# Seven block products in place of eight for the first sixteen tiles of a feed-forward's down projection

## The chip, the cores and the metric

One core of a Trainium2 chip runs the kernel. The metric is the device time of one execution in microseconds, the median of the runs.

## The reference

One layer of a streaming encoder on x of shape (1, 2048, 1024) in float32: two attention branches, their merge by gates, an output projection, and then the feed-forward that the change is about.

```python
h = _rmsnorm(x, norm1_g[layer])
proj = jnp.einsum('bsd,de->bse', h, w_in[layer])
...
x = x + jnp.einsum('bsd,de->bse', merged, w_out[layer])
h2 = _rmsnorm(x, norm2_g[layer])
ff = jax.nn.silu(jnp.einsum('bsd,df->bsf', h2, w_ffn_gate[layer])) * jnp.einsum('bsd,df->bsf', h2, w_ffn_up[layer])
x = x + jnp.einsum('bsf,fd->bsd', ff, w_ffn_down[layer])
```

D_MODEL is 1024 and D_FF is 2816, which is 22 tiles of 128. Branch B scores all keys for each query, keeps the 256 best and attends to these.

## The kernel before

The sequence is worked in four blocks of 512 rows (NB = 4, ROWS = 512), each four row tiles of 128 (JT = 4). First all four blocks go through `project` (the input projection, in jobs), then each block goes through its attention and its output jobs: branches ("br"), output projection ("wo"), feed-forward.

A **job** is one load of 512 KB of weights and the 24 matmuls that use it. The list JOBS fixes their order for all engines. SyncE loads each job's weights into one of two buffers WRAW. GpSimd splits them into a high and a low half, WHI and WLO (`split`), because every product is computed as three matmuls, high by high, high by low, low by high (the helper `three`). GpSimd may start a job's split when TensorE has finished the job two places before it. Values are split likewise: ScalarE writes the high half, VectorE the low half.

Every engine has its own queue of instructions, written out in the kernel, and takes them in that order: an instruction that waits holds all behind it on its engine.

In the feed-forward, for each tile i TensorE does the gate job "fg" and the up job "fu"; ScalarE applies silu to the first into SL, VectorE multiplies (ff_ready), ScalarE and VectorE split the result into FFhi and FFlo. The 22 tiles are three PARTS of 8, 8 and 6. After the tiles of a part come its down jobs "fd" (`rows`): the values are the stationary operand, and w_down moves in pieces of 512 columns. VectorE adds the sums from PSUM to X1 (`add_row`).

Between these, work for the next block is slipped in: `near` is its near attention, and `search` (VectorE) with `counts` (ScalarE) finds for each row of the next block the threshold of the 256 best scores bit by bit. One **search call** on VectorE takes the counts of the call before, sets the next threshold THR, and counts two of the four row tiles against it; ScalarE counts the other two at the same time. `look` and `next(found)` are such calls, and `search_slots` says how many stand where. A search takes 31 bits, and its calls fall into the output projection and the first two PARTS of the feed-forward of blocks 0, 1 and 2. The last block has no search and no near attention behind it.

In `project`, a scoring unit is two matmuls or four into one of two places of PSUM (LP), a ReLU by ScalarE into RB, and a multiply-add by VectorE. About one unit follows each job of the list SECOND, whose places are called s, from s = 5 on. TensorE must wait for the ReLU of the unit two before.

## Time and profile before

| what | value |
|---|---|
| three runs, us | 3197.46, 3198.58, 3198.94; median 3198.58 |
| span of the profiled execution, from its first to its last instruction | 3196.7 us |
| TensorE busy | 3156.0 us, 99% |
| VectorE, ScalarE, GpSimd busy | 57%, 44%, 64% |
| mean granted TensorE clock | 0.999 |
| matmuls in it | 15678 |

The page gives the span of the profiled execution and no time of its own beside it; the span is 1.9 us under the median of the runs. A busy share is an average over stages: an engine that is busy 57% of the time can still be what another one waits for at one place.

### The profile page before, as it was taken

To read this page: it belongs to the slowest core of one execution; us is meant where nothing else is said; L and a number is where in the kernel's file an instruction comes from. 1 tells how busy PE (TensorE), PEld (TensorE's weight loads), DVE (VectorE), ACT (ScalarE), POOL (GpSimd) and SP (SyncE) were. 2 spreads that over 40 slices of the span, in tenths; PEclk is the share of its full clock that TensorE was granted. 3 is DMA by queue.
4 is the path that set the end of the run, shared out by engine and by line. 5 is a ranking of instruction groups with operands and counts; after the bars stand their busy time and mean duration, and the time that the engine had idled before them with its cause. 6 is when DMAs were issued, how large, how long until landed. Compare 5 with 4: busy or idle time off the path is not lost.

```text
span 3196.7 us, 44024 instructions
## 1 busy us (share of the span) xinstructions
PE 3156.0 (99%) x15678; PEld 2655.0 (83%) x15678; DVE 1814.8 (57%) x3706; ACT 1420.8 (44%) x2589; POOL 2036.0 (64%) x2201
## 2 busy tenths in 40 slices
PE   9999999999999999999999999999999999999998
PEld 7888888878878888888888888988888799888887
DVE  3335546537565545557666666967868689521111
ACT  3324435435473534337354534837655378320001
POOL 5666766665556666764666676366767922666676
PEclk9999999999999999999999999999999999999999
DMA  5765455355615333331533334163333500533332
GB/s 152 198 167 172 119 154 157 103 157 163 209 35 182 102 112 107 108 125 57 201 104 116 103 102 138 28 238 103 98 109 112 171 23 17 180 91 99 95 103 99
DMA packets 464201, 392.59 MB, mean 123 GB/s; under 512 B 29264, under 2 KB 394064, under 8 KB 463344
## 3 DMA queue, kind: packets, MB, share of 16 engines
q1 hardware_dynamic: 442544, 345.56, 36.0%
q10 hardware_dynamic: 21440, 44.22, 3.7%
q8 instruction: 126, 2.06, 0.3%
q14 instruction: 91, 0.75, 0.1%
HBM read 323.76 MB, written 62.81 MB: 121 GB/s over the span
## 4 chain that ended last, share of the span: by engine, by line
PE 92%; POOL 2%; ACT 2%; DVE 2%; issue 1%; DMA 1%; SPq 0%; POOLq 0%; ACTq 0%; DVEq 0%
PE BANK L1049 22%; PE BANK L1051 21%; PE BANK L1050 21%; PE LP L1049 4%; PE LP L1051 4%; PE LP L1050 4%; PE BANK L1330 3%; PE BANK L1355 2%; PE LP L1166 2%; PE LP L1165 2%; PE LP L1310 2%; PE LP L1311 2%; PE BANK L1357 2%; POOL WLO L986 1%; POOL WHI L984 1%
## 5 line engine op out<-in xcount | busy, mean ns | idle before, releaser
L986 POOL TENSOR_TENSOR WLO<-WRAW,WHI 128x512 fp32r<-128x512 f32 x912 | 1213.3, 1330 | 76.0
L984 POOL TENSOR_SCALAR WHI<-WRAW 128x512 fp32r<-128x512 f32 x912 | 639.6, 701 | 776.1 <-PE BANK L1051 622.1
L1049 PE MATMUL BANK<-H2hi,WHI 128*128 128x512 f32 x1376 | 538.7, 392 | 1.1 <-POOL WLO L986 1.1
L1050 PE MATMUL BANK<-H2lo,WHI 128*128 128x512 f32 x1376 | 535.9, 389 | 0.0
L1051 PE MATMUL BANK<-H2hi,WLO 128*128 128x512 f32 x1376 | 535.8, 389 | 0.0
L1049 PE MATMUL BANK<-HThi,WHI 128*128 128x512 f32 (+1 forms) x1024 | 405.1, 396 | 0.8 <-DVE QS L2044 0.5
L1050 PE MATMUL BANK<-HTlo,WHI 128*128 128x512 f32 (+1 forms) x1024 | 399.4, 390 | 0.0
L1051 PE MATMUL BANK<-HThi,WLO 128*128 128x512 f32 (+1 forms) x1024 | 399.3, 390 | 0.0
L1751 ACT ACTIVATE MASK<-SCD,THR 128x896 bf16<-128x896 f32 (+5 forms) x186 | 281.9, 1516 | 191.8 <-DVE THR L2104 164.6
L1051 PEld LDWEIGHTS BANK<-H2hi,WLO 128*128 128x128 f32 x1376 | 258.3, 188 | 54.4
L1049 PEld LDWEIGHTS BANK<-H2hi,WHI 128*128 128x128 f32 x1376 | 258.6, 188 | 53.3 <-issue 1.3
L1050 PEld LDWEIGHTS BANK<-H2lo,WHI 128*128 128x128 f32 x1376 | 258.6, 188 | 51.1
L2071 DVE TENSOR_SCALAR_CACHE_REDUCE MASK<-SCD,THR 128x640 bf16<-128x640 f32 (+2 forms) x192 | 278.1, 1486 | 3.4
L1739 ACT ACTIVATE RB<-LP 128x1024 f32<-128x1024 f32 (+7 forms) x176 | 143.4, 819 | 231.9 <-PE LP L1166 207.9
L2525 DVE TENSOR_TENSOR BANK<-BANK,SL 128x512 f32<-128x512 f32 x88 | 61.2, 696 | 325.7 <-PE BANK L1051 305.9
L2308 DVE SCALAR_TENSOR_TENSOR SCP<-RB,IW,SCP 128x1024 f32<-128x1024 f32 (+7 forms) x140 | 175.2, 1266 | 106.2 <-ACT RB L1739 105.2
L1051 PEld LDWEIGHTS BANK<-HThi,WLO 128*128 128x128 f32 (+1 forms) x1024 | 190.9, 186 | 42.8
L2237 DVE TENSOR_TENSOR PTlo<-BANK,PThi 128x512 fp32r<-128x512 f32 (+1 forms) x296 | 193.2, 659 | 57.5 <-ACT PThi L1680 56.4
L1049 PEld LDWEIGHTS BANK<-HThi,WHI 128*128 128x128 f32 (+1 forms) x1024 | 191.1, 187 | 38.8 <-issue 0.6
L1050 PEld LDWEIGHTS BANK<-HTlo,WHI 128*128 128x128 f32 (+1 forms) x1024 | 191.3, 187 | 36.9
L1633 ACT ACTIVATE LGb<-LGb,NMB 128x1024 f32<-128x1024 f32 (+7 forms) x192 | 174.1, 907 | 57.9 <-POOL NMB L905 54.8
L905 POOL TENSOR_SCALAR NMB<-MXB 128x1 f32<-128x1 f32 x112 | 32.6, 291 | 250.6 <-DVE MXB L2194 247.6
(314 smaller groups left out, 6457.6 us busy)
## 6 DMA issues: line engine op xcount, KB each, us to landing
WRAW<-in_w_in SPq DMA_DIRECT2D x124, 512.0 KB, 4.2
WRAW<-in_w_ffn_gate SPq DMA_DIRECT2D x88, 512.0 KB, 3.8
WRAW<-in_w_ffn_up SPq DMA_DIRECT2D x88, 512.0 KB, 3.8
WRAW<-in_w_ffn_down SPq DMA_DIRECT2D x88, 512.0 KB, 3.5
qsp<-QS SPq DMA_DIRECT2D x32, 512.0 KB, 5.8
WRAW<-in_w_out SPq DMA_DIRECT2D x32, 512.0 KB, 4.6
gates<-GS ACTq DMA_DIRECT2D x62, 256.0 KB, 2.2
GL<-gates ACTq DMA_DIRECT2D x48, 256.0 KB, 4.5
```

Source lines behind the costliest of these rows:

```text
L984: nc.gpsimd.tensor_scalar(hi, raw, 1.0, 1.0, ALU.mult, ALU.mult).then_inc(w_hi, 1)
L986: nc.gpsimd.tensor_tensor(lo, raw, hi.bitcast(f32), ALU.subtract).then_inc(w_split, 1)
L1049: nc.tensor.matmul(dst, whi, mhi, start=first, stop=False)
L1050: nc.tensor.matmul(dst, whi, mlo, start=False, stop=False)
L1051: return nc.tensor.matmul(dst, wlo, mhi, start=False, stop=last)
L1330: last = nc.tensor.transpose(dst[:, 2 * e + h, :], probabilities(b, kind, p, h, t), IDENT[:, :])
L1633: nc.scalar.activation(lg, lg, ACT.Exp, bias=NMB[:, slot, 0:1], accum_out=(ES if s else RS)[:, j, h0:h0 + 1]).then_inc(probs, made(probs, ...
L1739: nc.scalar.activation(RB[:, g % 2, 0:w], logits(("idx",) + key)[:, 0:w], ACT.Relu).then_inc(relu_ready, made(relu_ready, key))
L1751: nc.scalar.activation(mask_of(b)[:, j, 0:w], found_at(b, j)[:, 0:w], ACT.Sign, bias=THR[:, j:j + 1].bitcast(f32), accum_out=CNT[:, j:j + ...
L2071: last = stepped(nc.vector.tensor_scalar(junk[:, j, 0:w], found_at(b, j)[:, 0:w], threshold(j), None, op, ALU.add, accum_out=CNT[:, j:j + 1]))
L2237: nc.vector.tensor_tensor(PTLO[b][r][:, 0:w, :], trans(key)[:, 0:w, :], PTHI[b][r][:, 0:w, :].bitcast(f32), ALU.subtract).then_inc(pt_read ...
L2308: ins = nc.vector.scalar_tensor_tensor(s, r, iw, s, ALU.mult, ALU.add)
```

## The change

It treats the down projection of tiles 0 to 15 as four **quads** of four tiles. In a quad, rows, tiles (even and odd) and columns each fall into two halves, and the 2 x 2 by 2 x 2 block product is formed by seven products in place of eight. Each product is 12 matmuls of the same shape as before. Tiles 16 to 21 keep the old way.

- The products are "11", "t1", "t2", "22", "t3", "21", "t4" in this order. Four of them ("t1" to "t4") use sums of blocks of w_down, which are the same for all four blocks of rows; the other three use w_down itself.
- The sums of weights are formed once, in `project(0)`: for each of eight pairs p of tiles, SyncE loads 1 MB of w_down into DRAW, VectorE forms four sums in DSUM (512 elements per partition each), ScalarE copies their high halves to DHI (2048 elements), VectorE writes the low halves DLO over DSUM, and ScalarE's queue sends both (1 MB each) to DRAM (tsum). The pairs stand at s = 6, 8, ... 20. Pair p + 1 waits for the writes of pair p (dsum_out).
- In the feed-forward the halves of the summed weights are loaded straight into WHI and WLO, 1 MB per product, with no split. A third pair of buffers WHI2, WLO2 is used by the jobs of tiles 0 to 15. Because of the region it lies in, its first split in a block waits for the last "wo" job.
- The sums of the values are formed on GpSimd (`form_sums`): one 256-wide sum for an even tile, three for an odd one. ScalarE and VectorE split these too (`high_parts`, `low_parts`).
- "11", "t2", "t3" and "t4" accumulate on top of one another in LP[0], and "22" on top of "t1" in two banks. VectorE adds each intermediate result to X1 before TensorE may go on with the next one: `down_quad` waits for down_added of "11" before "t2", of "t1" before "22", of "t2" before "t3", of "t3" before "t4".
- The search calls keep their number per part (14), and are placed anew.
- Some semaphores are merged.

```diff
+            def down_quad(b, quad):
...
+                    if x == "t2":
+                        pe.wait_ge(down_added, n(down_added, (b, quad, "11")))
+                        product(x, operand, chain, False)
+                    if x == "22":
+                        pe.wait_ge(down_added, n(down_added, (b, quad, "t1")))
+                        product(x, operand, corner, False)
+                    if x == "t3":
+                        pe.wait_ge(down_added, n(down_added, (b, quad, "t2")))
+                        product(x, operand, chain, False)
...
+                def add_quad(quad, part):
+
+                    add_banks(quad, "t1", (0, 2))
+                    look("fd", part)
+                    add_chain(quad, "t2")
+                    add_banks(quad, "22", (0, 2))
+                    add_chain(quad, "t3")
+                    add_banks(quad, "21", (1, 3))
+                    add_chain(quad, "t4")
...
                         near(b + 1, part_no, at_)
                         next(found, None)
                         near(b + 1, part_no, at_ + 1)
+                        if i // 4 < QUADS and i % 4 == 3:
+                            add_quad(i // 4, part)
```

```diff
+                if key[0] == "wo":
+                    last_out = i
+                third = key[0] == "fs" or key[0] in ("fg", "fu") and key[2] < PARTS[-1][0]
+                w = min((0, 1, 2) if third else (0, 1), key=lambda s: used[s])
+                slot.append(w)
+                before.append(max(used[w], last_out) if w == 2 else used[w])
```

```diff
+            def down_sums(p, step_):
+
+                if step_:
+                    dve.wait_ge(sum_hi, n(sum_hi, ("down", p)))
+                    nc.vector.tensor_tensor(DLO[:, :, :], DSUM[:, :, :], DHI[:, :, :].bitcast(f32), ALU.subtract
+                                            ).then_inc(sum_split, made(sum_split, ("down", p)))
+                    return
+                dve.wait_ge(const_in, n(const_in, ("down", p)))
+                if p:
+                    dve.wait_ge(dsum_out, 32 * p)
...
+                        act.wait_ge(sum_split, n(sum_split, ("down", p)))
+                        c = slice(p % 2 * ROWS, (p % 2 + 1) * ROWS)
+                        for i, half in enumerate((DHI, DLO)):
+                            act.dma_start(io["tsum"][p // 2, :, i, :, c].rearrange("t p c -> p t c"), half[:, :, :].bitcast(f32)
+                                          ).then_inc(dsum_out, 16)
```

The first place is VectorE's queue behind tile 3 of block 0, before the change. L2525 multiplies the up values by the silu, L2528 writes the low half, and the next five rows are a search call.

```order
L2525 TENSOR_TENSOR BANK<-BANK,SL 128x512 [waits silu_ready,bank_full]
L2528 TENSOR_TENSOR FFlo<-BANK,FFhi 128x512 [waits ff_hi]
L2097 TENSOR_SCALAR TAKE<-CNT 128x2 [waits topk_step]
L2101 TENSOR_SCALAR TAKE<-CNT 128x1 [waits tiles_counted]
L2101 TENSOR_SCALAR TAKE<-CNT 128x1
L2104 SCALAR_TENSOR_TENSOR THR<-TAKE,THR 128x4 [waits topk_step]
L2071 TENSOR_SCALAR MASK,CNT<-SCD,THR 128x640 [waits threshold_set]
L2071 TENSOR_SCALAR MASK,CNT<-SCD,THR 128x768
L2525 TENSOR_TENSOR BANK<-BANK,SL 128x512 [waits silu_ready,bank_full]
```

The same place after the change, from the last two 256-wide low halves on; X_237 is X1. L2789 adds LP ("11"), L2800 adds the banks ("t1").

```order
L2763 TENSOR_TENSOR FSlo<-FSUM,FShi 128x256 [waits sum_hi]
L2763 TENSOR_TENSOR FSlo<-FSUM,FShi 128x256
L2789 TENSOR_TENSOR X_237<-LP,X_237 128x2x512 [waits bank_full,rows_added]
L2768 TENSOR_TENSOR FSlo<-SL,FShi 128x512 [waits ff_hi]
L2300 TENSOR_SCALAR TAKE<-CNT 128x2 [waits topk_step]
L2304 TENSOR_SCALAR TAKE<-CNT 128x1 [waits tiles_counted]
L2304 TENSOR_SCALAR TAKE<-CNT 128x1
L2307 SCALAR_TENSOR_TENSOR THR<-TAKE,THR 128x4 [waits topk_step]
L2274 TENSOR_SCALAR MASK,CNT<-SCD,THR 128x640 [waits threshold_set]
L2274 TENSOR_SCALAR MASK,CNT<-SCD,THR 128x768
L2800 TENSOR_TENSOR X_237<-BANK,X_237 128x512 [waits bank_full,rows_added]
L2800 TENSOR_TENSOR X_237<-BANK,X_237 128x512
```

A whole search call now stands between the add of "11" and the add of "t1", and behind the add of "t1" stands a second one (the `look` of `add_quad`) before the add of "t2".

The second place is ScalarE's queue in `project(0)`, at s = 8 and 9 (pair p = 1), before the change: QS are heads of queries, RB the ReLU of a scoring unit.

```order
L1552 ACTIVATE QS_120<-BANK 64x512 [waits q_out0,bank_full]
L1552 ACTIVATE QS_120<-BANK 64x512
L1739 ACTIVATE RB<-LP 128x384 [waits logits_full,score_added]
L1552 ACTIVATE QS_121<-BANK 64x512 [waits q_out1,bank_full]
L1552 ACTIVATE QS_121<-BANK 64x512
L1739 ACTIVATE RB<-LP 128x384 [waits logits_full,score_added]
```

And after the change:

```order
L1718 ACTIVATE QS_120<-BANK 64x512 [waits q_out0,bank_full]
L1718 ACTIVATE QS_120<-BANK 64x512
L2030 CAST DHI<-DSUM 128x2048 [waits dsum_out,down_formed]
L1905 ACTIVATE RB<-LP 128x384 [waits logits_full,score_added]
L1718 ACTIVATE QS_121<-BANK 64x512 [waits q_out1,bank_full]
L1718 ACTIVATE QS_121<-BANK 64x512
L2036 DMA tsum<-DHI 128x4x512 [waits sum_split]
L2036 DMA tsum<-DLO 128x4x512
L1905 ACTIVATE RB<-LP 128x384 [waits logits_full,score_added]
```

The ReLU of each unit now stands behind the copy DHI, which waits for the DMA writes of the pair before, or behind the issue of the writes, which waits for VectorE's low half.

## Rows read from the trace of the kernel before

**Rows 1.** The page: busy time of each engine, and the chain that ended last.
```profile
PE 3156.0 (99%) x15678; PEld 2655.0 (83%) x15678; DVE 1814.8 (57%) x3706; ACT 1420.8 (44%) x2589; POOL 2036.0 (64%) x2201
...
PE 92%; POOL 2%; ACT 2%; DVE 2%; issue 1%; DMA 1%; SPq 0%; POOLq 0%; ACTq 0%; DVEq 0%
```

**Rows 2.** Timeline of TensorE in a down job: start us, us, what.
```profile
1154.74 0.39 PE L1049 MATMUL LP<-WHI,FFhi 128*128 128x512 f32 x1
...
1157.46 0.39 PE L1049 MATMUL BANK<-WHI,FFhi 128*128 128x512 f32 x1
```

**Rows 3.** Timeline where an up job of block 0 ends.
```profile
1101.40 0.39 PE L1049 MATMUL BANK<-H2hi,WHI 128*128 128x512 f32 x1
...
1101.60 0.70 DVE L2525 TENSOR_TENSOR BANK<-BANK,SL 128x512 f32<-128x512 f32 x1 [5.81 <-PE BANK L1051]
...
1102.34 0.59 ACT L1977 CAST FFhi<-BANK 128x512 fp32r<-128x512 f32 x1 [3.57 <-DVE BANK L2525]
```

**Rows 4.** Timeline of VectorE: a search call in block 2's feed-forward, then four adds.
```profile
2305.41 1.10 DVE L2097 TENSOR_SCALAR TAKE<-CNT 128x2 int32<-128x2 f32 x1
...
2306.86 1.95 DVE L2071 TENSOR_SCALAR_CACHE_REDUCE MASK<-SCD,THR 128x1664 bf16<-128x1664 f32 x1
...
2308.73 2.08 DVE L2071 TENSOR_SCALAR_CACHE_REDUCE MASK<-SCD,THR 128x1792 bf16<-128x1792 f32 x1
...
2310.73 2.48 DVE L2470 TENSOR_TENSOR X<-LP,X 128x512 f32<-128x512 f32 x4
```

**Rows 5.** Groups by shape on VectorE: count, busy us, mean ns, idle before.
```profile
L2308 DVE SCALAR_TENSOR_TENSOR SCP<-RB,IW,SCP 128x1024 f32<-128x1024 f32 x70 | 101.1, 1445 | 71.3 <-ACT RB L1739 71.1
...
L2071 DVE TENSOR_SCALAR_CACHE_REDUCE MASK<-SCD,THR 128x1280 bf16<-128x1280 f32 x31 | 47.8, 1542 | 0.0
...
L2071 DVE TENSOR_SCALAR_CACHE_REDUCE MASK<-SCD,THR 128x1152 bf16<-128x1152 f32 x31 | 43.8, 1413 | 1.1
...
L2071 DVE TENSOR_SCALAR_CACHE_REDUCE MASK<-SCD,THR 128x768 bf16<-128x768 f32 x31 | 31.3, 1008 | 0.0
L2071 DVE TENSOR_SCALAR_CACHE_REDUCE MASK<-SCD,THR 128x640 bf16<-128x640 f32 x31 | 27.3, 880 | 1.1
...
L2308 DVE SCALAR_TENSOR_TENSOR SC<-RB,IW,SC 128x384 f32<-128x384 f32 x7 | 10.2, 1462 | 22.7 <-ACT RB L1739 22.6
```

**Rows 6.** Groups by shape on GpSimd: a 256-wide sum.
```profile
L921 POOL TENSOR_TENSOR XZ<-XZ,OTB 128x256 f32<-128x256 f32 x12 | 8.8, 737 | 0.0
```

**Rows 7.** Groups by shape on ScalarE: the widest count, and a 256-wide cast.
```profile
L1751 ACT ACTIVATE MASK<-SCD,THR 128x2048 bf16<-128x2048 f32 x31 | 61.6, 1988 | 0.0
...
L1680 ACT CAST PThi<-BANK 128x256 fp32r<-128x256 f32 x32 | 11.6, 363 | 1.4 <-PE BANK L1330 1.4
```

**Rows 8.** Timeline around the first gate job of block 0, GpSimd and TensorE.
```profile
1033.16 0.62 POOL L984 TENSOR_SCALAR WHI<-WRAW 128x512 fp32r<-128x512 f32 x1 [4.22 <-PE BANK L1051]
...
1035.98 1.30 POOL L986 TENSOR_TENSOR WLO<-WRAW,WHI 128x512 fp32r<-128x512 f32 x1
...
1037.96 0.36 PE L1498 MATMUL BANK<-H2hi,WHI 128*128 128x256 f32 x1 [0.47 <-DVE H2lo L2499]
```

**Rows 9.** The page: ScalarE's DMA queue, and its issues of 256 KB.
```profile
q10 hardware_dynamic: 21440, 44.22, 3.7%
...
gates<-GS ACTq DMA_DIRECT2D x62, 256.0 KB, 2.2
```

**Rows 10.** Windows, 140 to 160 us: the last two are DMA share, GB/s.
```profile
140.00:160.00 20.00, 20.00 (x90) 16.61 (x90) 6.59 (x7) 7.02 (x11) 14.58 (x15) 1.00 0.68 172
```

**Rows 11.** Timeline of block 0's projection: VectorE at s = 6, ScalarE at s = 22.
```profile
99.79 0.41 DVE L2383 TENSOR_TENSOR VBS<-BANK,VBS 128x256 fp32r<-128x256 f32 x1
...
192.78 0.60 ACT L1739 ACTIVATE RB<-LP 128x512 f32<-128x512 f32 x1 [4.81 <-PE LP L1166]
```

**Rows 12.** Windows, the idle end of TensorE: the granted clock is third from the end.
```profile
3190.00:3196.00 6.00, 0.00 (x0) 0.00 (x0) 1.40 (x3) 0.85 (x2) 2.00 (x2) 0.73 0.87 347
```

More of the change, by code:

```diff
@@ L1066, in job @@
                         beside(s)
-                    last = three(dst, WHI[i % 2][:, s, 0:width], WLO[i % 2][:, s, 0:width], mhi[:, s, :], mlo[:, s, :],
+                    last = three(dst, WHI[SLOT[i]][:, s, 0:width], WLO[SLOT[i]][:, s, 0:width], mhi[:, s, :], mlo[:, s, :],
                                  s == 0, s == k - 1)
@@ L1520, in _ @@
                             job(H2hi, H2lo, (silu_ready, (b, i)), beside=beside, ring="pair")
-                        job(H2hi, H2lo, (ff_split, (b, i)), beside=beside_up, ring="pair")
-                    if part is PARTS[-1] and b + 1 < NB:
+                        kept_for = (ff_ready if i // 4 < QUADS else ff_split, (b, i))
+                        job(H2hi, H2lo, kept_for, beside=beside_up, ring="pair")
+                        if i % 4 == 3 and i // 4 < QUADS:
+                            down_quad(b, i // 4)
+                    if part is not PARTS[-1]:
+                        pass
+                    elif b + 1 < NB:
                         ahead[0] = attend(b + 1)
@@ new lines, in add_banks @@
+                def add_banks(quad, x, banks):
+                    top, half = X1ROWS[x]
+                    done_, what = added_before(quad, x)
+                    dve.wait_ge(done_, n(done_, what))
+                    dve.wait_ge(bank_full, n(bank_full, ("fs", b, quad, x)))
+                    for r, bk in enumerate(banks):
+                        c = X1[:, 2 * top + r, half * ROWS:(half + 1) * ROWS]
+                        last = nc.vector.tensor_tensor(c, BANK[bk][:, :], c, ALU.add)
+                    last.then_inc(down_added, made(down_added, (b, quad, x)))
@@ L2536, in _ @@
                         near(b + 1, part_no, at_ + 3)
-                    for half in range(D // ROWS):
-                        if half == 0 or part is not PARTS[-1]:
+                    for half in range(D // ROWS) if part is PARTS[-1] else ():
+                        if half == 0:
                             look("fd", part, half)
```

350 lines of the change are left out of this document (282 added, 68 removed).

## The prediction

> **What bounds the kernel now.** I read the page first: TensorE is busy 99% of the span and carries 92% of the chain that ended last [rows 1]. So work taken from TensorE is worth its full issue time, and any wait given to it costs its full length; no other queue hides either. Then I read the timeline for what a matmul costs. A 512-wide one lasts 0.39 us by its row, but they are pipelined: from 1154.74 to 1157.46 lie 12 intervals, so one is issued every 0.227 us [rows 2]. The reader must use the interval, not the duration. Last I read how other engines answer TensorE. VectorE's multiply starts 0.2 us after the next job's first matmul (1101.40 to 1101.60), and ScalarE's cast starts 0.04 us after that multiply has ended [rows 3].
>
> **The matmuls removed.** An eight-product quad has 96 matmuls, seven products have 84. Four quads in four blocks save 16 x 12 = 192 matmuls, 192 x 0.227 = **43.5 us**. This is the whole gain: nothing else on TensorE gets shorter. A product of 12 is 2.72 us, where a job was 24 matmuls or 5.44 us, so each hand-over in a quad has half the cover that one had.
>
> **The quads.** Let t = 0 be the start of "11", when the up job of the quad's last tile has ended. Without waits "t1" starts at 2.7, "t2" at 5.4, "22" at 8.2, "t3" at 10.9.
>
> VectorE multiplies from 0.2 to 0.9. GpSimd forms three sums of 256 elements, 0.74 each [rows 6], done at 3.2. ScalarE casts the last two (some 0.6, as the cast of 512 in [rows 3]) by 3.9, VectorE makes their low halves (512 elements together, about 0.7) by 4.65, and only then stands the add of "11". Four adds of 512 take 2.48, so one add of a pair takes 1.24 [rows 4]: it ends at 5.9 and "t2" waits 0.5. The low halves have both inputs in SBUF. A multiply-add with two inputs from SBUF took 1462 ns at 384 elements, as much as 1445 ns at 1024 [rows 5]: something other than length delays the short ones, by up to about 1 us. I take 0.4 of such delay here, so the wait is 0.9. In the last block this is all: 4 x 0.9 = 3.6 us.
>
> The Trainium skill ("SBUF — State Buffer", Who interferes with whom) says that a VectorE instruction with two SBUF inputs is shut out while a GpSimd instruction that reads SBUF runs. By it the delay would be up to one low half of a weight split on GpSimd, 1.3 us, and the quads' sum would rise by some 14 us; the rows agree in kind.
>
> In blocks 0 to 2 VectorE then has the low halves of 512 (0.65), a search call, and the add of "t1". The call's small steps take from 0.8 to 1.45 us (2305.41 to 2306.86) [rows 4]; I take 0.8. Its two counts take c = 1.9 us in block 0 (640 and 768 wide), 3.0 in block 1 (1152 and 1280) [rows 5], 4.0 in block 2 (1664 and 1792) [rows 4]. From the start of "t2" that is 0.65 + 0.8 + c + 1.3, against the 2.72 of "t2": "22" waits c. From there stands the second call and the add of "t2", 0.8 + c + 1.27, against the 2.72 of "22": "t3" waits c - 0.65. "t4" has two products of cover and waits for nothing. A quad thus costs 0.9 + c + c - 0.65 = 0.25 + 2c: 4.05, 6.25 and 8.25 us. Four each are 74.2, with the last block **78 us**. Low end: no delay on the port, some counts of ScalarE's side early, 65. High end: small steps of 1.45, full port delay, a late start where near attention stands ahead, 100.
>
> **The first gate job.** Its split started at 1033.16 and ended at 1037.3, and TensorE began at 1037.96 [rows 8]. Now the split waits for the last "wo" job, which ends just ahead of 1037.96. Half a split is 2.0 us, and the late row scaling on GpSimd stands behind the whole split, ahead of the second transposes: 2.3 us a block, **9 us**. It is 5 if the second half and the scaling are hidden by the half-width matmuls.
>
> **The sums of weights.** This is a ring: DMA writes of pair p end, four sums on VectorE, copy of 2048 on ScalarE, ReLU, one scoring unit on VectorE, low half of 2048, writes of p + 1. The sums are 512 wide, 0.62 to 1.5 each; 0.8 by the nearest full-width rows. The copy is 2.0, as the 2048-wide count [rows 7]; ReLU 0.5; the unit 1.5 [rows 5]; the low half four times 0.62 to 1.0, taken as 2.6; hand-overs 0.3. Together 10.1 us, at least 8.9. The writes are 2.1 MB. ScalarE's queue moved 44.22 MB in 3.7% of the span, 118 us, or 374 GB/s, and lands 256 KB in 2.2 us, of which 0.7 are transfer [rows 9]: 1.5 + 5.6 = 7.1 us alone. But the DMA engines are 68% busy at this place already [rows 10], and at half of their time left the transfer is 11.2. I take 9.2. The ring is C = 19.3 us, between 16 and 26.
>
> TensorE's pace there is one job with its unit in 5.9 us, 11.8 for a pair. It can be ahead of ScalarE by the two places in LP only. The first pair's sums start at 100.2, behind VBS; ScalarE reaches the ReLU of s = 20 at 100.2 + 7C + 5.9. TensorE may not begin the unit of s = 22, whose ReLU stood at 192.8 [rows 11], so its matmuls at 192.4, before that. The delay is 7C - 86.3: **49 us** at C = 19.3, 26 at 16, 96 at 26.
>
> **What is hidden.** The 1 MB loads of summed weights have at least two products or one job of cover, 5.4 us, which the stretched quads lengthen. GpSimd gets one split less and 6 us of sums in each quad; with 4 us a split it has 11 of them in 62 us of TensorE. If that cover went, each late load would cost its excess over 5.4.
>
> **Sum.** 3196.7 - 43.5 + 78 + 9 + 49 = 3289 of span, and the runs are 1.9 above: **3291 us**.
>
> **Rivals.**
> - *The weight ring is hidden* (0.12): DMA faster than its rows and SBUF sums short. For it: TensorE does not read tsum for 800 us. Against: ScalarE and VectorE stop in order, and even C = 16 is above 11.8. Then -43.5 + 78 + 9: 3242.
> - *The search calls don't stand in the way* (0.07): VectorE passes the adds early enough and only the first wait remains. Against: the order of its queue. -43.5 + 14 + 9 + 49: 3227.
> - *Faster* (0.10): the returns from VectorE to TensorE are covered, in block 0 as in the quads, so that the 192 matmuls count in full: -43.5 + 9, 3164. It decides when all waits together are under 43.5 us, 2.7 per quad with none in `project(0)`. For it speaks that VectorE is busy only 57% [rows 1]; against it that the waits are set by one place, not by the share.
> - *The clock falls* (0.08): at the idle end of the kernel the mean granted clock is 0.73 [rows 12], so it falls to 1.2 GHz after TensorE has stood still. Two gaps a quad in blocks 1 and 2 would put 16 products at half rate, 16 x 2.7 = 43 us: 3334. Against it: gaps here are 2 to 4 us between busy stretches.
> - *Nothing measurable* (0.03): waits of about 43 us by chance.
>
> The Trainium skill ("TensorE: Matmul & The Clock Gate", HAM oscillation — how this bites in real kernels) says that idle gaps between bursts of matmuls put the clock to half again and again. By that rule the fourth rival holds; the trace has too few gaps to show it.
>
> **How the numbers follow.** The forecast has 0.60, with a range of its own from 3251 (-43.5 + 65 + 5 + 26) to 3362 (-43.5 + 100 + 10 + 96.5). The range of 3225 to 3365 takes in most of it, the first and fourth rival and half of the second, 0.8 in all. 0.2% is about what a measurement of this kernel can tell from no change. Faster 0.10, same 0.03, slower 0.87.
>
> **What would show it.** TensorE's matmuls: 192 fewer. Waits of TensorE for X1 written by VectorE at L2789 and L2800, 0.9 us ahead of "t2" in all blocks, and growing from block 0 to 2 ahead of "22" and "t3", gone in block 3. VectorE in a search call while TensorE stands. A gap of 2 us ahead of each first gate job, ended by WLO. In `project(0)`, TensorE waiting for RB, ScalarE's DHI spaced by 19 us and each ended by a DMA or DSUM. I am wrong if DHI comes every 12 us, or if the adds of "t1" end within 8 us of the quad's start in block 2.

## The result and the profile after

The changed kernel took **3516.08 us** (median of 4 runs, 3507.76 to 3518.43) against 3198.38 (3197.46 to 3198.94): ratio 1.0988, 95% interval 1.0973 to 1.1004. It is slower by 318 us where 92 were forecast. The profiled execution, the fastest of the four, has a span of 3505.9 us, 309.2 more than before; the accounts below are of this one.

The page of the changed kernel, to be read against [rows 1]: busy time, granted clock in 40 slices, chain that ended last.

```profile
PE 3213.3 (92%) x15486; PEld 2672.1 (76%) x15486; DVE 2054.0 (59%) x3970; ACT 1472.9 (42%) x2693; POOL 2081.9 (59%) x2265
...
PEclk9889999999999999999989999999998899999999
...
PE 65%; DVE 11%; POOL 7%; issue 6%; ACT 6%; DMA 4%; ACTq 0%; SPq 0%; POOLq 0%; DVEq 0%
```

192 matmuls are gone, as forecast. Yet TensorE is busy 57.3 us longer. Without the removed 43.5 us it should have been busy 3112.5, so 100.8 us are matmuls at a lower clock. Idle time rose from 40.7 to 292.6 us, by 251.9. Together 251.9 + 100.8 - 43.5 = 309.2, the whole difference. So 100.8 us of it are not idle time but slow running. At the full rate not all of this would come back: some slow products run while the next one could not start anyway, as is shown below.

What TensorE waited for (us, times, longest), over the whole span:

```profile
PE LP L1162 <- DVE X L2789: 65.2, 23, 7.7
PE LP L1608 <- DVE NPlo L2476: 56.4, 6, 13.3
PE BANK L1162 <- POOL WLO L1069: 37.7, 7, 9.6
PE BANK L1162 <- DVE FSlo L2759: 15.1, 9, 4.2
PE BANK L1162 <- DVE X L2800: 14.5, 8, 3.2
PE BANK L1162 <- ACT SL L2173: 12.0, 4, 6.0
PE LP L1162 <- DVE MX L2463: 11.9, 3, 6.5
...
PE BANK L1659 <- POOL WLO L1069: 9.2, 5, 2.2
```

The first, fifth and last are waits that I had priced (L2789 adds "11", "t2", "t3" and "t4", L2800 adds "t1", L1659 is the first gate job). The others are not in the forecast: NPlo stands between the quads, FSlo is a low half that "t1" waits for, MX and SL are near attention's masks and a silu that come so late that "11" and "t1" find their places in PSUM still in use.

**Where it lies.** I take VectorE's multiply of each tile as a clock mark and measure from the first to the last of a block. "Quads" is the sum of the four intervals that span a quad's products (in the kernel before, the same four intervals hold its down jobs). "Between" is the sum of the other 12 intervals among tiles 0 to 15. All in us, worked out from the start times in the timelines.

| kernel | median | first multiply | feed-forward, blocks 0 to 3 | quads | between |
|---|---|---|---|---|---|
| before | 3198.4 | 1054.3 | 330.1, 335.7, 342.8, 315.5 | 131.0, 130.3, 130.1, 130.6 | 141.4, 142.2, 142.3, 130.6 |
| changed | 3516.1 | 1128.9 | 377.8, 413.5, 446.2, 314.2 | 147.9, 161.5, 170.8, 129.2 | 172.2, 188.8, 205.1, 130.6 |

A quad's removed matmuls are 2.72 us, so four intervals without any new loss would be 10.9 shorter than before. The account, in the forecast's own terms:

| term | forecast | measured |
|---|---|---|
| matmuls removed | -43.5 | -43.5 |
| quads | +78 | 27.8 + 42.1 + 51.6 + 9.5 = +131.0 |
| between the quads | 0 | 30.8 + 46.6 + 62.8 + 0 = +140.2 |
| first gate jobs (block 0's taken to be like block 1's) | +9 | 2.0 + 2.0 + 2.5 + 2.3 = +8.8 |
| sums of weights, `project(0)` | +49 | 74.6 - 2.0 = +72.6 |
| sum | +92.5 | +309.1 |

Block 3, with no search and no near attention behind it, gained 1.3 us. By blocks, the quads were forecast at 16.2, 25.0, 33.0 and 3.6 us. In blocks 0 to 2 both the quads and what lies between them were longer than before.

**Between the quads.** The kernel before, VectorE behind tile 1 of block 0: the last row is where near attention's masks begin.

```profile
1066.10 0.70 DVE L2525 TENSOR_TENSOR BANK<-BANK,SL 128x512 f32<-128x512 f32 x1 [6.79 <-PE BANK L1051]
1067.45 0.69 DVE L2528 TENSOR_TENSOR FFlo<-BANK,FFhi 128x512 fp32r<-128x512 f32 x1 [0.65 <-ACT FFhi L1977]
1068.06 0.33 DVE L2260 CUSTOM_DVE_ANT_0 NLG<-LP,TABA,SINK 64x128 f32<-64x128 f32 x1
```

The same place of the changed kernel, by engine:

```profile
1142.41 0.69 DVE L2821 TENSOR_TENSOR SL<-BANK,SL 128x512 f32<-128x512 f32 x1 [2.46 <-ACT SL L2173]
...
1144.52 0.50 DVE L2759 TENSOR_TENSOR FSlo<-FSUM,FShi 128x256 fp32r<-128x256 f32 x1 [1.41 <-ACT FShi L2156]
1146.30 2.31 DVE L2763 TENSOR_TENSOR FSlo<-FSUM,FShi 128x256 fp32r<-128x256 f32 x2 [1.28 <-ACT FShi L2158]
1148.53 1.74 DVE L2768 TENSOR_TENSOR FSlo<-SL,FShi 128x512 fp32r<-128x512 f32 x1
1150.20 0.33 DVE L2463 CUSTOM_DVE_ANT_0 NLG<-LP,TABA,SINK 64x128 f32<-64x128 f32 x1
...
1153.47 0.69 DVE L2476 TENSOR_TENSOR NPlo<-LP,NPhi 128x512 fp32r<-128x512 f32 x1
...
1143.18 0.73 POOL L1116 TENSOR_TENSOR FSUM<-SL 128x256 f32<-128x256 f32 x1 [3.14 <-DVE SL L2821]
...
1163.63 1.04 POOL L1075 TENSOR_TENSOR NLG<-NLG,RS 128x512 f32<-128x512 f32 x1 [11.53 <-DVE RS L2484]
...
1147.58 0.39 PE L1164 MATMUL BANK<-H2hi,WLO 128*128 128x512 f32 x1
1154.31 0.55 PE L1608 MATMUL LP<-NPhi,NV 128*128 128x256 f32 x1 [6.33 <-DVE NPlo L2476]
...
1155.30 0.63 PE L1162 MATMUL BANK<-H2hi,WHI 128*128 128x512 f32 x1
1155.72 0.63 PE L1163 MATMUL BANK<-H2lo,WHI 128*128 128x512 f32 x1
...
1159.12 0.39 PE L1162 MATMUL BANK<-H2hi,WHI 128*128 128x512 f32 x1
1159.35 0.40 PE L1163 MATMUL BANK<-H2lo,WHI 128*128 128x512 f32 x1
```

The masks (L2260, now L2463) began 1.96 us after the start of the multiply before, and begin 7.79 us after it now: VectorE goes GpSimd, ScalarE, VectorE and back for each group of sums, and two of its own 256-wide subtractions take 1.15 us each. NPlo comes last, and TensorE stands 6.33 us for it. Then the matmuls start 0.43 us apart, not 0.23, for some 4 us. The same wait was 13.3 us at one place of block 2. GpSimd, in the middle of a weight split, stands 11.5 us, since its share of near attention (L1075) waits for VectorE too.

**A quad of block 2.** Forecast: waits of 0.9 ahead of "t2", 4.0 ahead of "22", 3.35 ahead of "t3". Timeline of the changed kernel, VectorE and then TensorE, from the first matmul of "11" on:

```profile
2463.26 0.68 DVE L2821 TENSOR_TENSOR SL<-BANK,SL 128x512 f32<-128x512 f32 x1
...
2467.12 2.29 DVE L2763 TENSOR_TENSOR FSlo<-FSUM,FShi 128x256 fp32r<-128x256 f32 x2 [1.28 <-ACT FShi L2158]
2469.33 1.21 DVE L2789 TENSOR_TENSOR X<-LP,X 128x1024 f32<-128x1024 f32 x1
...
2475.44 1.28 DVE L2800 TENSOR_TENSOR X<-BANK,X 128x512 f32<-128x512 f32 x2
...
2459.80 0.80 PE L1162 MATMUL LP<-WHI,FShi 128*128 128x512 f32 x1 [6.52 <-DVE MX L2463]
...
2470.60 0.79 PE L1162 MATMUL LP<-WHI,FShi 128*128 128x512 f32 x1 [3.04 <-DVE X L2789]
2471.19 0.63 PE L1163 MATMUL LP<-WLO,FShi 128*128 128x512 f32 x1
...
2476.78 0.50 PE L1162 MATMUL BANK<-WHI,FShi 128*128 128x512 f32 x1 [0.69 <-DVE X L2800]
2477.11 0.40 PE L1163 MATMUL BANK<-WLO,FShi 128*128 128x512 f32 x1
...
2483.44 0.79 PE L1162 MATMUL LP<-WHI,FShi 128*128 128x512 f32 x1 [3.66 <-DVE X L2789]
```

TensorE had ended tile 3's up job at 2453.3 (6.52 us before 2459.80), and VectorE multiplies at 2463.26: it is 10 us late when the quad begins, from what stood between. The three waits that I had forecast add up to 7.4 us, against 8.25. But "t2" ran from 2470.60 to some 2475.9 at half rate, 5.3 us for 12 intervals where "22" took 2.7, and the first half of "11" and of "t3" ran at half rate too. The slow "t2" hid most of the wait of "22": in the next quad, where "t2" ran at full rate from 2556.42 on, "22" waited 3.16 us and not 0.69.

Ahead of "t2" TensorE waits 3.02 to 3.04 us in each quad of block 0, and 1.98 in each of block 3. In block 0 the first matmuls behind the wait still come 0.23 to 0.39 us apart. Then they come 0.43 apart, in the first quad from the third on, in the second from the seventh on (intervals of 0.43 show as durations of 0.63). In block 3 all 12 keep their rate:

```profile
1186.00 0.50 PE L1162 MATMUL LP<-WHI,FShi 128*128 128x512 f32 x1 [3.02 <-DVE X L2789]
...
1186.72 0.63 PE L1164 MATMUL LP<-WHI,FSlo 128*128 128x512 f32 x1
...
1256.68 0.50 PE L1162 MATMUL LP<-WHI,FShi 128*128 128x512 f32 x1 [3.04 <-DVE X L2789]
...
1258.27 0.63 PE L1162 MATMUL LP<-WHI,FShi 128*128 128x512 f32 x1
...
3190.43 0.50 PE L1162 MATMUL LP<-WHI,FShi 128*128 128x512 f32 x1 [1.98 <-DVE X L2789]
```

The three waits of all quads, taken from the timeline: ahead of "t2" 12.1, 10.7, 10.6 and 7.9 us in blocks 0 to 3, 41.3 together where 14.4 were forecast; ahead of "22" 0, 6.8, 7.7 and 0, 14.5 where 35.6 were forecast; ahead of "t3" 3.9, 6.6, 13.3 and 0, 23.9 where 27.8 were forecast. They add up to 79.7, close to the 78 of the forecast, but that is luck: the first is nearly three times its forecast and the second less than half. Some 50 us more are waits ahead of "11" and of "t1", which were not in it at all.

**VectorE's room.** Windows over the feed-forward of blocks 0 and 2, of the kernel before: the third pair of figures is VectorE's busy time, the third from the end the granted clock.

```profile
1054.30:1384.40 330.10, 330.10 (x1515) 274.76 (x1515) 183.89 (x484) 133.76 (x256) 233.94 (x240) 1.00 0.36 110
...
2199.70:2542.60 342.90, 340.19 (x1554) 281.88 (x1554) 261.04 (x485) 186.29 (x256) 253.99 (x246) 1.00 0.37 114
```

And of the changed kernel:

```profile
1128.90:1506.70 377.80, 336.34 (x1467) 273.11 (x1467) 233.30 (x540) 143.23 (x280) 243.97 (x254) 0.96 0.42 133
...
2404.40:2850.50 446.10, 360.12 (x1506) 287.52 (x1505) 311.54 (x540) 196.12 (x280) 262.86 (x260) 0.90 0.37 118
```

In block 2 VectorE now has 311.5 us of work, and TensorE needs 343 - 10.9 = 332: 94% of that time is taken. In block 0 it is 233.3 of 319 (73%), in block 1 by the same reckoning 272.7 of 325 (84%), in block 3 93.0 of 305 (31%). Quads and the stretches between them together lost 58.6, 88.7, 114.4 and 9.5 us. So the loss grows with the load, and the page's 59% does not show that; but there is no threshold in it, as block 0 lost much with a quarter of VectorE's time free.

### The profile page after: what moved, and what is told of

Its sections match the earlier page's. It is cut to its first block, busy times and chain, and to the rows that moved or that the text cites. A ratio compares the mean times of both kernels' runs of the same rounds, so it can differ in the third digit from the quotient of the medians.

```text
span 3505.9 us, 44511 instructions
## 1 busy us (share of the span) xinstructions
PE 3213.3 (92%) x15486; PEld 2672.1 (76%) x15486; DVE 2054.0 (59%) x3970; ACT 1472.9 (42%) x2693; POOL 2081.9 (59%) x2265
## 4 chain that ended last, share of the span: by engine, by line
PE 65%; DVE 11%; POOL 7%; issue 6%; ACT 6%; DMA 4%; ACTq 0%; SPq 0%; POOLq 0%; DVEq 0%
PE BANK L1162 14%; PE BANK L1164 14%; PE BANK L1163 14%; PE BANK L1491 3%; POOL WLO L1069 3%; PE LP L1162 3%; DMA tsum<-DLO 2%; PE LP L1164 2%; PE LP L1163 2%; DVE MASK L2274 2%; PE BANK L1516 2%; PE LP L1471 2%; PE LP L1472 2%; POOL WHI L1067 2%; PE LP L1327 2%
## 5 line engine op out<-in xcount | busy, mean ns | idle before, releaser
L1069 POOL TENSOR_TENSOR WLO<-WRAW,WHI 128x512 fp32r<-128x512 f32 x880 | 1180.6, 1342 | 73.4
L1067 POOL TENSOR_SCALAR WHI<-WRAW 128x512 fp32r<-128x512 f32 x880 | 625.2, 710 | 739.0 <-PE BANK L1164 429.9
L1162 PE MATMUL BANK<-HThi,WHI 128*128 128x512 f32 (+1 forms) x1024 | 413.4, 404 | 45.0 <-POOL WLO L1069 36.8
L2173 ACT ACTIVATE SL<-BANK 128x512 f32<-128x512 f32 x88 | 52.1, 592 | 349.5 <-PE BANK L1164 342.7
L1162 PE MATMUL LP<-WHI,FShi 128*128 128x512 f32 x256 | 116.1, 454 | 88.0 <-DVE X L2789 65.2
```

The costliest lines, as they stand in the source:

```text
L1067: nc.gpsimd.tensor_scalar(hi, raw, 1.0, 1.0, ALU.mult, ALU.mult).then_inc(w_hi, 1)
L1069: nc.gpsimd.tensor_tensor(lo, raw, hi.bitcast(f32), ALU.subtract).then_inc(w_split, 1)
L1162: nc.tensor.matmul(dst, whi, mhi, start=first, stop=False, skip_group_check=chained)
```

## The experiments

Each was timed against the kernel before on the same chip (3198.5 to 3198.8). Differences below are of medians, to 3516.1, where nothing else is said. The kernels that leave `project(0)` alone have their first multiply between 1127.9 and 1133.8 us, so a few us there say nothing.

**1. The ring of weight sums.** Three kernels.

```diff
+# e1_loads_scalare: in ScalarE's queue, behind its wait for pair p; SyncE's load_down for p > 0 gone
+    act.dma_start(DRAW[:, :, :], weights(io["w_ffn_down"][0], (2 * p + 2, 2 * p + 3), 0, D)).then_inc(const_in, 16)
```

> The loads of w_down for pairs 1 to 7 of the weight sums are issued by ScalarE behind its wait for the pair before, so that SyncE's queue no longer waits for these sums in project(0); the ring of sums, copy, low half and writes stays as it is. Theory A (TensorE's 36.8 us of waits for WLO come from SyncE standing in the wait of load_down with the weight loads behind it): these waits vanish, part of the half-rate matmuls with them, the last gate sigmoid of block 0 comes 35 to 55 us earlier, about 3465 in all. Rival B (the ring stops ScalarE and VectorE in order, and TensorE's waits only change their name to RB and GS): the stage stays within 10 us, 3506 to 3520.

```diff
+# e7_writes_cut: tsum has 128 columns in place of 1024; read into WHI, WLO likewise
-    c = slice(p % 2 * ROWS, (p % 2 + 1) * ROWS)
+    c = slice(p % 2 * 64, (p % 2 + 1) * 64)
```

> Of the summed weights only one eighth of the bytes is written in project(0) and read in the feed-forward; the rest of WHI and WLO keeps older weights, so that the products t1 to t4 are others than the reference's. All instructions and waits stay. Theory D (the writes are the largest part of the ring, some 9 of its 22 us): the copies of DHI come every 13 us, TensorE's waits for WLO, GS and RB nearly vanish, and the first multiply of block 0 comes 60 us earlier. Rival E (the ring is long through its eight instructions on VectorE and ScalarE and the units between them): every 18 us or more, at most 30 us earlier. The feed-forward's stages stay within 2 us if the 1 MB loads are hidden; 3455 by D.

```diff
+# e12_half_pairs: the conditions on s of all engines
-    (s - DOWN_SLOT) % 2 == 0
+    (s - DOWN_SLOT) % 4 == 0
```

> The changed kernel, with sums of weights for four pairs of tiles in place of eight, at s = 6, 10, 14, 18, twice as far apart; quads 2 and 3 read those of quads 0 and 1, so the output is not the reference's. Theory C (the loss in project(0) is the ring's length of 22 us against the 11.8 that TensorE needs for two jobs; at a distance of 23.6 us it is hidden): the first multiply of block 0 comes at 1062 or earlier in place of 1129, 3450. Rival E (each pair costs TensorE its share, some 9 us, wherever it stands, since ScalarE and the DMA engines stop for it): half of the loss stays, 1092, 3480.

| kernel | median | first multiply | DHI to DHI, mean of the intervals |
|---|---|---|---|
| changed | 3516.1 | 1128.9 | 22.0 |
| e1_loads_scalare | 3500.2 | 1116.5 | 20.1 |
| e7_writes_cut | 3484.6 | 1102.2 | 18.2 |
| e12_half_pairs | 3457.6 | 1068.3 | not compared |

In the changed kernel SyncE's queue waits 100.7 us in `load_down` with the weight loads behind it, and within 80 to 280 us TensorE waits for weights:

```profile
PE BANK L1162 <- POOL WLO L1069: 36.8, 6, 9.6
...
SPq L859 <- DVE DSUM L2538: 100.7, 7, 16.2
```

With the loads on ScalarE's queue the same stretch reads:

```profile
PE LP L1327 <- ACT RB L1906: 44.8, 7, 15.3
```

So the blocked queue was real, but it was mainly where the wait showed: taken away, most of the wait moves to RB, as the forecast had it, and 12.4 us come back. Theory A, with 35 to 55, falls; rival B, with at most 10, is nearer. The ring itself, from the timeline of the changed kernel:

```profile
149.94 2.29 DVE L2526 TENSOR_TENSOR DLO<-DSUM,DHI 128x2048 fp32r<-128x2048 f32 x1
164.55 0.83 DVE L2533 TENSOR_TENSOR DSUM<-DRAW 128x512 f32<-128x512 f32 x1 [12.32 <-DMA tsum<-DLO]
```

Here 12.3 us lie between the end of the low half and the next sums. The means over the seven pairs behind the first are 13.8 for this (in the first two ScalarE comes 4 us late to issue the writes), 2.9 for the four sums, 1.9 for the copy and 3.4 for ReLU, scoring unit and low half: 22.0. Writing an eighth of the bytes shortened the ring only to 18.2: the 13.8 became 9.1 and VectorE still waited up to 8.6 us for the writes, so most of this leg is not bytes, and rival E holds. At twice the distance (23.6 us for a ring of 22) all but 12 of the 72.6 us are gone: theory C holds nearly in full.

The forecast's formula for the delay, 7C - 86.3, can now be tried with each measured ring C: it gives 67.7 for the changed kernel, 54.5 for e1 and 40.8 for e7, and 72.6, 60.2 and 45.9 were found. It is some 5 us short each time and follows the ring each time. So the 12.4 us of e1 are those of its shorter ring, not a second loss beside it; why the ring got shorter there was not looked into. In e7 the loads of the summed weights in the feed-forward have an eighth of their bytes too, and its four stages together are within 2 us of the changed kernel's (380.2, 408.9, 448.6, 315.4): these loads were hidden, as forecast.

**2. The search calls between the adds.**

```diff
+# e2_calls_behind, VectorE only
-    look("fd", part)          # in add_quad, behind the adds of "t1"
...
-    next(found, None)
+    if not closes:            # closes: the last tile of a quad
+        next(found, None)
...
     add_quad(i // 4, part)
+    next(found, None)
+    look("fd", part)
```

> VectorE's two search calls of each quad stand behind the quad's adds; nothing else moves. Theory S (the calls between the adds are the price of the quads, as I had reckoned it, 2c each): the waits at L2800 go, 12 quads times 3.8, 6 or 8 us in blocks 0, 1, 2, 71 us in all, 3445. Rival L (VectorE is late everywhere in these blocks, from its load and its waits for sums; a call moved behind the quad makes the next tile late): under 30 us, 3490 or more.

3477.4 us, 38.7 less (27.7 between the profiled executions). Quads 144.3, 152.2, 159.8, 129.4: only 23.7 us less in all where I had reckoned 71. Theory S falls, and rival L is nearer. The waits at L2800 went, but the wait for NPlo rose from 56.4 to 65.3 us, and the wait ahead of "t2" stayed.

**3. The sums of the values.** Left out (e3), or formed by VectorE (e6).

```diff
+# e3_no_sums (ScalarE; VectorE likewise; form_sums gone)
-    nc.scalar.copy(FShi[:, kk, 4:6, :], FSUM[:, 1:3, :])
+    nc.scalar.copy(FShi[:, kk, 4:6, :], SL[:, 1, :].rearrange("p (s r) -> p s r", s=2))
+# e6_sums_vectore (VectorE, behind its multiply; form_sums gone from GpSimd)
+    nc.vector.tensor_tensor(FSUM[:, 0, :], ev[:, high], bk[:, high], ALU.add)
+    nc.vector.tensor_tensor(FSUM[:, 1, :], FSUM[:, 0, :], ev[:, low], ALU.subtract)
+    nc.vector.tensor_tensor(FSUM[:, 2, :], bk[:, low], FSUM[:, 1, :], ALU.subtract)
```

> GpSimd's four sums of the values per pair of tiles are left out: ScalarE and VectorE split parts of the values themselves instead, so that the products t1 to t4 are formed from other values than the reference's; the number and shape of all other instructions stay. Theory G (the way over GpSimd, three dependent sums of 0.74 us and two hand-overs, and its reads beside VectorE's subtractions, make each odd tile some 4 to 6 us late on VectorE, and the splits too): in each feed-forward 8 odd tiles times 3 to 5 us, above all the waits at L2789 (65 us) and FSlo (15 us), block 3's stage 8 to 10 us shorter (304 to 306), and 80 to 120 us in all, 3400 to 3435. Rival S (search calls): the first wait of each quad alone, 0.9 us each, 15 us, 3500.

3420.6 us, 95.5 less, as theory G said. Between the quads 154.7, 165.9, 186.2: 59.3 us back. Block 3's quads fell from 129.2 to 120.8, against 119.7 without any loss: there the sums were 8.4 of the 9.5 us lost.

> VectorE forms the sums of the values right behind its multiply, GpSimd forms none; the result is the reference's. Theory H (the price is the hand-over: GpSimd reaches the sums late, between weight splits, takes 0.74 us for each and delays VectorE's 256-wide subtractions to 1.2 us; on VectorE four sums take some 0.45 us each, 116 us of work in all four blocks but no wait): block 3's stage falls by 4 us to 310, the three others by 10 to 15 each, 3475. Rival V (VectorE is the engine without room, and 29 us more of work per block makes blocks 1 and 2 longer): 3520 to 3560.

3463.6 us, 52.5 less, a little more than theory H said, though VectorE has more work. Groups by shape on VectorE (count, busy us, mean ns, idle before), of the changed kernel:

```profile
L2763 DVE TENSOR_TENSOR FSlo<-FSUM,FShi 128x256 fp32r<-128x256 f32 x64 | 73.5, 1186 | 41.0 <-ACT FShi L2158 41.0
...
L2759 DVE TENSOR_TENSOR FSlo<-FSUM,FShi 128x256 fp32r<-128x256 f32 x32 | 15.9, 497 | 52.2 <-ACT FShi L2156 52.2
```

And with the sums on VectorE:

```profile
L2743 DVE TENSOR_TENSOR FSlo<-FSUM,FShi 128x256 fp32r<-128x256 f32 x64 | 39.4, 655 | 6.0 <-ACT FShi L2128 6.0
...
L2739 DVE TENSOR_TENSOR FSlo<-FSUM,FShi 128x256 fp32r<-128x256 f32 x32 | 26.3, 823 | 0.0
```

The two subtractions of L2763 took 1186 ns each where GpSimd's weight split begins right behind its sums (in the timeline above: 1146.30, with the split from 1145.59 on), and 655 with the sums on VectorE. L2759, beside GpSimd's own 256-wide sums, took 497. Single rows show what makes the difference. In the changed kernel all 64 of L2763 overlap a weight split (822 to 1565 ns). With the sums on VectorE 35 of the 64 overlap nothing on GpSimd and take 410 to 426 ns; those that lie beside the split's low half alone (WLO, both inputs in SBUF) take 1.5 us, and those beside its high half alone (WHI, one input) 0.42.

But this is not what gave the 52.5 us. L2739, which is L2759's place, went from 497 to 823 ns, and all low halves of values and sums together took 152.8 us in place of 166.6, while the four sums came on top with 85.4 us. What went is the waiting: the idle time before L2763 fell from 41.0 to 6.0 us, and before all these low halves from 129.1 to 6.6.

**4. The load of the counts.** The counts narrowed on VectorE and on ScalarE, so that the calls keep their small steps and waits.

```diff
+# e4_narrow_counts
-    w = width_of(b, j)
+    w = NARROW if b else width_of(b, j)          # ScalarE; NARROW is 128
...
-    w = width_of(b, j)
+    w = width_of(b, j) if isinstance(threshold(j), float) or op is ALU.is_gt or not b else NARROW   # VectorE
```

> In the searches for blocks 1 to 3 each count looks at 128 scores in place of 640 to 2048, on VectorE and ScalarE, so that the thresholds are not the reference's; the calls, their small steps and waits stay. Theory V (VectorE's own load: with the counts it is busy 311 of the 332 us that TensorE needs in block 2, so that nothing late can be caught up): blocks 0, 1, 2 fall from 378, 413 and 446 us to one level of about 340 each, 200 us or more in all, 3310. Rival G (the sums' way over GpSimd sets each tile's end): the three blocks fall to block 0's level at best, 378 each, 100 us, 3415.

3356.3 us, 159.8 less. The three blocks come to nearly one level, 357.2, 361.0 and 367.2 (the kernel before grows as much, from 330.1 to 342.8), so the growth from block to block was the counts. But the level is not 340: between the quads 152.5, 151.6, 151.2 remain against 142, and the quads take 147.0, 146.2 and 145.8, some 27 us over a quad stage without loss. Both were partly right: V in the growth and the size, G in what is left. The edit cannot tell the two engines apart: in block 2 VectorE's busy time fell from 311.5 to 211.0 us and ScalarE's from 196.1 to 112.7. That it is VectorE's load which counts is argued from its being the fuller one, and not shown.

**5. Near attention ahead.**

```diff
+# e5_near_ahead, odd tiles of quads; ScalarE likewise ahead of high_parts
+    near(b + 1, part_no, at_)
     low_parts(i)
-    near(b + 1, part_no, at_)
```

> Behind an odd tile the step of near attention (ScalarE's NPhi, VectorE's masks and NPlo) stands ahead of the split of that tile's values and sums in place of behind it. Theory N (between the quads TensorE stands for NPlo, 56 us in all, because the way mult, GpSimd's sums, ScalarE's casts, VectorE's low halves ends 6 us later than the old split and holds VectorE's queue): these waits go but for some 10 us, with half-rate matmuls behind them about 60 us, 3455. Rival Q (the same lateness only moves on: the low halves of the odd tile, the quad's first wait or the next silu come late by what near attention takes, 4 us): under 20 us, 3500.

3507.2 us, 8.9 less, no more than the 10.7 us over which the changed kernel's own runs spread: rival Q. TensorE's waits of this kernel:

```profile
PE LP L1162 <- DVE X L2792: 74.1, 26, 7.7
...
PE LP L1608 <- DVE NPlo L2479: 34.4, 5, 12.0
```

The wait for NPlo shrank by 22.0 us and that for the adds grew by 8.9. Here the order within a late queue mostly chose who is late.

**6. All four, and the calls placed anew.** e8 has e1, e2, e5 and e6 together; e9 adds:

```diff
+# e9_calls_placed (search_slots; add_quad; behind add_quad)
-    return 1 if at_ - part[0] in ((2, 3, 6, 7), (0, 3, 4, 7), (0, 1))[PARTS.index(part)] else 2
-    return 3 - at_ if phase == "wo" else 2 if last else 1
+    return 1 if not last or at_ - part[0] in (0, 1) else 2
+    return 3 - at_ if phase == "wo" else 2 if last else 3
...
     add_chain(quad, "t3")
+    next(found, None)
...
-    next(found, None)
     look("fd", part)
```

> The loads of w_down on ScalarE's queue, the search calls behind the quads' adds, near attention's step ahead of an odd tile's split, and the sums of the values on VectorE, all together. If the four delays are separate places, the gains add up: 16 + 39 + 60 + 35, about 3365. If they are one chain that runs out of room on VectorE, the sum is less than half of that, 3430 or more. Either way it stays slower than before.

> All four edits of the run before, and the seven search calls of a quad placed anew: one behind each of tiles 0, 1 and 2 in place of 2, 2, 1, one between the adds of t3 and 21, three behind the quad. Theory P (between the quads VectorE has 10.9 us for a tile, and two calls of 5 us in block 2 with a multiply and the low halves are more than that; there the 12 intervals took 161, 178 and 193 us against 141 of the kernel before): they fall to about 150 each, and as four calls now follow the quads these grow by 5 to 8 us per quad in block 2 and hardly in block 0: 3389 less some 50, 3340. Rival R (VectorE and ScalarE have no room anywhere, work moved is time moved): within 20 of 3389.

e8 took 3389.4 us, 126.7 less; the four gains alone make 15.9 + 38.7 + 8.9 + 52.5 = 116.0. They add up, as separate delays would; the 3365 expected for that case had 60 for near attention's step, which alone gave 8.9. e9 took 3367.5 (ratio 1.0525, 1.0509 to 1.0541), the fastest version that leaves nothing out, and still slower than before. Between the quads it is at 146.8, 150.6, 155.9, 79.1 us less than e8, as theory P had it, but its quads took 55.6 more. The 21.9 us that are left lie nearer to rival R (within 20) than to P (some 50): most of the work moved was time moved.

**7. Only the calls' new places, in the kernel before.**

```diff
+# e10_before_placed: search_slots as in the change
-    return 1 if at_ - part[0] in ((0, 1, 2, 3, 4, 6), (0, 1, 2, 3, 4, 6), (0, 1))[PARTS.index(part)] else 2
+    return 1 if at_ - part[0] in ((2, 3, 6, 7), (0, 3, 4, 7), (0, 1))[PARTS.index(part)] else 2
-    return 3 - at_ if phase == "wo" else 2 if last else 3 - 2 * at_
+    return 3 - at_ if phase == "wo" else 2 if last else 1
```

> The kernel before, and of the change only the places of the search calls: two behind tiles 0, 1, 4, 5 of the first part and one behind the others, one in each half of the down jobs. Theory P: the two calls make VectorE late here too, in blocks 1 and 2, by some 3 us per pair of such tiles: 3215 to 3230. Rival I (alone they are covered, since the multiply and one low half leave 9.5 us of each 10.9; only together with the sums' way does it get late): within 5 us of before, 3195 to 3203.

3221.0 us against 3198.5, ratio 1.0070 (1.0057 to 1.0082): theory P. The stage grew by 0.1, 6.1 and 16.2 us in blocks 0, 1, 2. Of a part's 14 calls 12 instead of 10 now stand behind tiles and 2 instead of 4 in the down jobs. Two lines of the change that I had passed over as "placed anew" cost 22.5 us by themselves. Two waits of TensorE that the kernel before did not have are 14.2 of them:

```profile
PE LP L1439 <- POOL NLG L992: 8.8, 4, 3.7
PE LP L1447 <- DVE NPlo L2273: 5.4, 4, 2.6
```

**8. What is left.** e11 is e8 with e4; e13 is e3 with e4; e14 is e13 with e2. Their edits are the ones shown, put together.

> All four edits and the counts over 128 scores, so that the thresholds are not the reference's. If VectorE's counts are all that is left of the loss in the feed-forward, blocks 0 to 2 come to what block 3 takes plus the matmuls of near attention, 322 us each, quads 122 and between them 142: 3389 - 29 - 57 - 92, about 3215. Rival (near attention's chain over four engines is late by itself behind the sums): 335 to 345 each, 3260.

> Counts over 128 scores and no sums of the values, both left out of the changed kernel together; the output is not the reference's. The 12 intervals between the quads took 172, 189 and 205 us against 142 before; without the sums alone 155, 166, 186, with narrow counts alone 152, 152, 151. Theory T (the 140 us lost there are these two together and nothing else): both left out bring them to 141 to 143. Rival (a third part, near attention over four engines or the third pair of buffers): 146 or more in each block. The whole: 3516 - 95 - 160 if they add up, 3261; some 20 more if each takes the same lateness, 3280.

> As the run before, and VectorE's two search calls of a quad behind its adds. Theory T: then nothing but the first wait of each quad is left, quads of block 3's length without sums, 121 us, in all blocks, and the feed-forward comes to 321 in blocks 0 to 2: under 3240. Rival: the narrow calls cost little between the adds, and the quads stay at 130 or more because of near attention's steps in them.

| kernel | median | feed-forward, blocks 0 to 3 | quads | between, blocks 0 to 2 |
|---|---|---|---|---|
| e11_all_narrow | 3283.0 | 335.5, 343.5, 353.8, 306.6 | 135.4, 135.0, 135.9, 121.7 | 146.8, 146.8, 146.8 |
| e13_narrow_no_sums | 3298.8 | 339.2, 343.5, 350.7, 312.0 | 137.0, 134.2, 134.5, 127.0 | 144.5, 146.0, 145.9 |
| e14_also_behind | 3284.2 | 333.0, 338.5, 350.2, 307.5 | 132.2, 132.2, 133.1, 122.5 | 146.2, 144.5, 146.0 |

e11 took 3283.0, beyond the 3260 of its rival and far from the 3215: counts are not all that is left. In e13, with sums and counts out of the way, 10.5 of the 140.2 us between the quads remain: the two together explain 129.7. Theory T asked for 141 to 143 and its rival for 146 or more; at 144.5 to 146.0 there is a third part, of 3 to 4 us a block. Taken out one by one sums and counts gave 59.3 and 110.8, more than 129.7 together, since either removes some of the same lateness. The whole kernel, at 217.3 us less, stayed 38 us short of 95.5 + 159.8.

For the quads theory T was too bold: some 132 in place of 121 (e14). The rest, some 3 us a quad, is only in blocks with near attention and a search behind them; which of their small steps it is, stays open. e14 did not come under 3240: its three blocks took 333.0, 338.5 and 350.2 where 321 each were reckoned, 59 us more. Some 13 of these are in the reckoning: without any loss the kernel before's stages would be 319.2, 324.8 and 332.0 long.

## Why the prediction was wrong, step by step

- **The sign and the gain were right.** 192 matmuls fewer, -43.5 us; the kernel is slower.
- **First gate jobs: right in size, partly by luck.** 9 forecast, 8.8 found, with waits for WLO of 2.2 us. These are some 1.8 more than the 0.5 before, and in block 1 the first 14 matmuls behind the wait came 0.21 us apart and not 0.12, which the forecast did not have.
- **The sums of weights: mechanism right, size off.** 49 forecast, 72.6 found, inside the bounds of 26 to 96. The mis-sized term is C, 19.3 forecast and 22.0 measured, and in it the writes: 13.8 from the low half to the next sums where I took 9.2, while the engines' own steps took 8.2 and not 10.1. 7C - 86.3 gives 67.7 for the measured C. The upper bound of 26 for C had no terms behind it.
- **The quads: 78 forecast, 131 found.** The step "ends at 5.9 and 't2' waits 0.5", with 0.4 of delay added, was mis-sized: the wait is 1.98 in block 3 and about 3 in most quads of blocks 0 to 2. In block 3 the quad ran by the forecast's own times up to the casts; then the two low halves took 2.30 us and not 0.7 with a delay of 0.4. The Trainium skill ("SBUF — State Buffer", Who interferes with whom) says that a VectorE instruction with two inputs in SBUF contends with a GpSimd instruction that reads SBUF, and that the lock is exclusive. The 1.5 us beside a split's low half, against 0.42 with GpSimd idle, agree; the 497 ns beside GpSimd's sums and the 0.42 us beside a split's high half do not show it. The waits ahead of "22" were less than half of their forecast, and in block 0 there were none; those ahead of "t3" were 23.9 for 27.8. That the three waits came to the forecast's 78 all the same is luck. Two terms were missing: the half-rate products (up to 2.6 us each), and the lateness that VectorE and ScalarE bring along (FSlo 15.1, MX 11.9, SL 12.0 us).
- **Between the quads: 0 forecast, 140 found. This is the step that failed.** The passage "What is hidden" costed GpSimd's sums by GpSimd's room alone, and put the stretches between the quads at nothing. I counted who does the work and not who waits for it: ScalarE waits for the sums, VectorE for ScalarE, and behind VectorE stand near attention, the calls and the next multiply. The sums' way (59.3, e3) and the counts (110.8, e4), which met the same lateness, make 130 of the 140 together (e13). The calls' new places cost 22.5 us by themselves in the kernel before (e10); how much of the 140 they are was not tried. The load of VectorE in block 2 was 261.0 of 343 us already before the change, with more work to come: I read its 57% over the span only.
- **The clock was no rival but a companion.** I gave it 0.08 and 43 us, with "gaps here are 2 to 4 us" against it. It took 100.8 us: behind many gaps of 2 to 13 us in blocks 0 to 2 and in `project(0)` matmuls ran 0.43 us apart, at the 1.2 GHz level, where it is 0.23 at 2.4. The granted clock was 0.90 in the feed-forward of block 2, 0.86 between 80 and 280 us, and 1.00 in the feed-forward of block 3. The Trainium skill ("TensorE: Matmul & The Clock Gate", HAM oscillation — how this bites in real kernels) says that idle gaps between bursts bring the clock down again and again. The trace agrees by these figures, though not for the four gaps of 1.98 us in block 3. I should have charged the slow matmuls to the waits of the forecast and not to a case of their own.
- **The signs I named.** VectorE in a search call while TensorE stands: seen ahead of "22" and "t3" in blocks 1 and 2, in block 0 ahead of "t3" of one quad only. The 2 us gap: seen. DHI at 19 us: 22. RB as TensorE's wait: 6.9 us in the changed kernel, where SyncE's queue made most of it WLO, and 44.8 in e1.

## What to carry to other kernels

When a change sends a result over one more engine, price the way and not the work: write down what the receiving engine has queued behind its wait, and measure that engine's busy time against the time of the bounding engine *in that stage*. Here the loss of a feed-forward was 36 to 38 us with VectorE's share at 61 to 64% (e4), 59 at 73%, 89 at 84% and 114 at 94%. Reckon with slow matmuls behind expected gaps of TensorE of some microseconds as well. And treat "the same calls at other places" as a change with a price of its own.

## What was unexpected of the hardware

- Half the rate behind short gaps, and not by the gap alone, nor at once. After 6.33 us of standing, matmuls came 0.43 us apart for about 4 us. After 3.02 us at 1186.00 they fell to half rate from the third on and after 3.04 us at 1256.68 from the seventh on. After 3.04 us at 2470.60 all of "t2" ran at half rate; there TensorE had also stood 6.52 us some 11 us earlier. After 3.04 us at 1873.81 and 1.98 us at 3190.43 all 12 kept their rate. What decides it was not tried.
- From the end of a low half to the sums that wait for its writes, 2 MB in two transfers, lay 11.8 to 16.9 us, while loads of 1 MB and 512 KB ran beside them; with an eighth of the bytes it was still 8.6 to 9.7 us.
- The 256-wide subtraction with both inputs in SBUF took 0.42 us with nothing on GpSimd beside it, 0.42 beside the high half of a weight split, 0.50 beside GpSimd's 256-wide sums and 1.5 where it lay beside a split's low half alone.
